# Transformer layer on one core: first modulation rows, dense weight chunks, decay vectors and norm vectors laid out by the host as one run per partition

## What is computed

```python
mod = silu(c) @ w_mod + b_mod                    # (1024) @ (1024, 6144), for c and c_ctx
sh1, sc1, g1, sh2, sc2, g2 = split(mod, 6)
h = ln_plain(x) * (1 + sc1) + sh1                # needs the first 2048 columns of w_mod
qa, ka, va, ra, af, ab, qd, kd, vd, ga, gb = split(h @ w_in)        # w_in (1024, 8224)
log_f = log_sigmoid(af @ w_alpha_f + b_alpha_f) / 16                # and the same backwards
# gated linear attention and differential attention side by side,
# merged = sigmoid(ga) * (o_a @ w_proj_a) + sigmoid(gb) * (o_d @ w_proj_b)
x = ln(alpha * x + g1 * (merged @ w_out))
# then 16 SwiGLU experts (2816 wide), each choosing its tokens
```

## Time and profile before

| | |
|---|---|
| median of 3 runs | 1785.42 us (1784.49 to 1785.57) |
| the profiled execution | 1784.7 us, of it span 1782.9 us |
| TensorE matmul busy | 1657.5 us, 93% of the span |
| VectorE, ScalarE, GpSimd busy | 512.3, 301.4, 56.1 us |
| moved by DMA | 638.74 MB, mean 358 GB/s; sync queue 54736 packets, GpSimd queue 3744 |
| granted TensorE clock | 0.98 of full speed |

### The profile page before, as it was taken

The page is one execution under the profiler, slowest core; times in us unless marked ns, Lnnn a source line. Parts: engine busy times, 40 slices in busy tenths (PEclk is TensorE's granted clock), DMA queues, the critical chain, the costliest instruction groups (busy, mean ns, idle before and its releaser), DMA issues.

```text
span 1782.9 us, 19120 instructions
## 1 busy us (share of the span) xinstructions
PE 1657.5 (93%) x7934; PEld 776.9 (44%) x7934; DVE 512.3 (29%) x979; ACT 301.4 (17%) x647; POOL 56.1 (3%) x91
## 2 busy tenths in 40 slices
PE   6999999999999999898988989898988989898997
PEld 3767777778873333332323232332323232333332
DVE  4575647765771111010101011010101011011041
ACT  3543354563331000000000000000000000000100
POOL 3110000021000000000000000000000000000000
PEclk9999999999999999999999999999999999999999
DMA  9962232237599999999999999999999999999997
GB/s 346 364 229 101 78 127 101 86 111 256 218 388 422 402 421 430 439 429 430 436 433 423 435 433 434 431 430 437 428 437 424 435 433 431 433 433 434 427 427 323
DMA packets 58528, 638.74 MB, mean 358 GB/s; under 512 B 5233, under 2 KB 5417, under 8 KB 36209
## 3 DMA queue, kind: packets, MB, share of 16 engines
q1 hardware_dynamic: 54736, 629.83, 84.4%
q0 software_dynamic: 3744, 8.26, 1.5%
HBM read 634.17 MB, written 3.90 MB: 358 GB/s over the span
## 4 chain that ended last, share of the span: by engine, by line
PE 57%; DMA 38%; SPq 2%; ACT 1%; DVE 1%; issue 0%; POOL 0%; POOLq 0%; ACTq 0%; DVEq 0%
PE banks L1401 25%; DMA ring<-in_w_exp_gate 19%; PE banks L970 18%; DMA ring<-in_w_exp_up 17%; PE banks L1536 3%; PE banks L1383 2%; DMA ring<-in_w_exp_down 2%; PE banks L968 1%; SPq L595 1%; DMA ring<-in_w_mod 1%; PE banks L921 1%; PE banks L1165 1%; PE banks L979 1%; PE banks L1186 1%; PE banks L966 1%; PE banks L1122 1%
## 5 line engine op out<-in xcount | busy, mean ns | idle before, releaser
L1401 PE MATMUL banks<-ring,O 128*64 128x512 f32 (+1 forms) x2844 | 635.0, 597 | 74.9 <-DMA ring<-in_w_exp_gate 53.4
L1401 PEld LDWEIGHTS banks<-ring,O 128*64 128x64 f32 x2844 | 199.1, 139 | 513.5 <-issue 413.4
L1536 PE MATMUL banks<-ring,O 128*64 128x512 f32 x1400 | 304.6, 593 | 7.5 <-ACT O L1884 6.7
L2459 DVE TENSOR_TENSOR X<-X,banks 128x512 f32<-128x512 f32 x90 | 61.8, 687 | 612.0 <-PE banks L1383 612.0
L970 PE MATMUL banks<-slot_parts,X_parts 128*128 128x512 f32 x672 | 191.1, 405 | 0.0
L1536 PEld LDWEIGHTS banks<-ring,O 128*64 128x64 f32 x1400 | 101.6, 137 | 199.4 <-issue 193.5
L970 PEld LDWEIGHTS banks<-slot_parts,X_parts 128*128 128x128 f32 x672 | 119.8, 188 | 32.3 <-issue 10.7
L1879 ACT ACTIVATE O<-banks 128x512 f32<-128x512 f32 (+1 forms) x48 | 23.7, 563 | 645.1 <-PE banks L1401 645.1
L2015 DVE TENSOR_TENSOR slot_parts<-ring,slot_parts 128x512 fp32r<-128x512 f32 x168 | 106.2, 694 | 14.1 <-ACT slot_parts L1591 13.7
L970 PE MATMUL banks<-slot_parts,H_parts 128*128 128x512 f32 x384 | 106.9, 391 | 0.0
L1591 ACT ACTIVATE O<-banks 128x128 f32<-128x128 f32 (+3 forms) x51 | 22.4, 439 | 494.5 <-PE banks L1312 388.9
(11 more groups left out here) (348 smaller groups left out, 1173.1 us busy)
## 6 DMA issues: line engine op xcount, KB each, us to landing
ring<-in_w_exp_up SPq DMA_DIRECT2D x26, 5632.0 KB, 28.5
ring<-in_w_exp_down SPq DMA_DIRECT2D x26, 4096.0 KB, 25.0
ring<-in_w_exp_gate SPq DMA_DIRECT2D x13, 5632.0 KB, 27.6
ring<-in_w_exp_gate SPq DMA_DIRECT2D x13, 4224.0 KB, 26.3
ring<-in_w_exp_down SPq DMA_DIRECT2D x15, 3072.0 KB, 22.5
ring<-in_w_in SPq DMA_DIRECT2D x16, 2048.0 KB, 8.8
ring<-in_w_exp_up SPq DMA_DIRECT2D x8, 2816.0 KB, 23.9
N<-in_w_exp_gate SPq DMA_DIRECT2D x15, 1408.0 KB, 30.4
```

The lines of the kernel that those rows point to most:

```text
L1401: x = pe.matmul(banks[64 * w:64 * w + 64, 3 * m + b, 0:(i1 - i0) * P], xeT[:, 2 * (k % 4) + k // 4, :], w4[:, w, i0 * P:i1 * P], start=(k ...
L1536: x = pe.matmul(banks[64 * w:64 * w + 64, (4 if last else 6) + dc, :], hidT[:, i, 64 * w:64 * w + 64], rows[:, w, dc * BANK:(dc + 1) * BAN ...
L2459: dve.tensor_tensor(dst, dst, banks[:, 3 + n % 3 if spread or last else 6 + n % 2, :], ALU.add).then_inc(acc_done, 1)
```

## The change

The host lays arrays out anew before the kernel is called (this is no part of the device time), and the loads read them so:

- first modulation rows: `w_mod0`, per half and partition one run in the order of the k-tiles; 4 loads of 1024 KB (runs of 8 KB) and 2 of 2048 KB (runs of 16 KB) take the place of 16 loads of 512 KB. The waits stand where they stood, with new counts;
- weight chunks: `w_chunks`, per chunk and partition one run of 16 KB;
- decay weights: `w_ab`, one run of 1 KB per partition in place of 8 of 128 bytes;
- decay biases: `b_alpha`, one load of 128 runs of 32 bytes in place of two loads;
- norm vectors: a run of 8 bytes and of 4 bytes per partition;
- the pieces read a `w_mod` without its first 2048 columns (row distance 16 KB in place of 24 KB); their runs stay 8 KB.

The order of all loads, their destinations and all arithmetic are as before.

```diff
@@ -269,8 +268,11 @@
         wpart = [x[:].rearrange("p (k n) -> p k n", k=KT) for x in slots_r]
 
 
+        def mod0_at(half, k):
+            return (2 * UNIT if half else WS0 + 2 * KT * BANK) + k * D
+
         def mod0_rows(half, k):
-            return reg((2 * UNIT if half else WS0 + 2 * KT * BANK) + k * D, D).rearrange("p (w n) -> p w n", w=2)
+            return reg(mod0_at(half, k), D).rearrange("p (w n) -> p w n", w=2)
 
         def tile_of(x, k):
             return x[:, k * BANK:(k + 1) * BANK]
@@ -556,9 +558,7 @@
                 eng.wait_ge(out, f[0] // 2 + n + 1)
 
         def w_chunk(n):
-            kind, c0 = WCHUNKS[n]
-            w = {"in": w_in, "pa": w_pa, "pb": w_pb, "out": w_out}[kind]
-            return w[0].rearrange("(k p) n -> p k n", p=P)[:, :, c0:c0 + BANK]
+            return w_chunks[n].rearrange("p (k n) -> p k n", k=KT)
 
         def wait_loaded(eng, n):
             eng.wait_ge(wsem[PAIR[n]], 16 * (len(before_in_pair(n)) + 1))
@@ -590,12 +590,12 @@
             sp.dma_start(x_r[:, 0, :], x_prompt[0]).then_inc(ld_x[0], 16)
             sp.dma_start(x_r[:, 1:3, :], x_sample[0].rearrange("(t p) d -> p t d", p=P)).then_inc(ld_x[1], 16)
 
-            def load_mod0(half, k):
-                rows0 = w_mod[0, k * P:(k + 1) * P, 0:2 * D].rearrange("p (w h n) -> p w h n", w=2, h=2)
-                sp.dma_start(mod0_rows(half, k), rows0[:, :, half, :]).then_inc(ld_mod0[half][k // (4 if half else 2)], 16)
-
-            for k in range(KT):
-                load_mod0(0, k)
+            def load_mod0(half, i):
+                n = 4 if half else 2
+                sp.dma_start(reg(mod0_at(half, i * n), n * D), w_mod0[half][:, i * n * D:(i + 1) * n * D]).then_inc(ld_mod0[half][i], 16)
+
+            for i in range(4):
+                load_mod0(0, i)
 
             def load_chunk(n):
                 if n == 0:
@@ -615,7 +615,7 @@
                     n = i % len(piece)
                     if i >= len(piece):
                         sp.wait_ge(piece_used, i - len(piece) + 1)
-                    sp.dma_start(piece[n], w_mod[0, k * P:(k + 1) * P, 2 * D * (b + 1):2 * D * (b + 2)]).then_inc(ld_piece[n], 16)
+                    sp.dma_start(piece[n], w_mod[k * P:(k + 1) * P, 2 * D * b:2 * D * (b + 1)]).then_inc(ld_piece[n], 16)
 
             def gate_up(w, e, q):
                 return gate_v[w][e].rearrange("(p k) f -> p k f", p=P)[:, 2 * q:2 * q + 2, :]
@@ -624,8 +624,8 @@
                 sp.dma_start(first_ups[k], gate_up(1, 0, 3)[:, k, :]).then_inc(land_u[3], 16)
 
             load_chunk(0)
-            for k in range(KT):
-                load_mod0(1, k)
+            for i in range(2):
+                load_mod0(1, i)
             load_pieces(0, 2)
             load_chunk(1)
             load_pieces(2, 6)
@@ -814,18 +814,17 @@
                     q = 32 * (2 * w + c)
                     pool.dma_start(mod_bias[0][q:q + 2, :].rearrange("p (h n) -> p h n", h=2),
                                    b_mod[:, w * D:(w + 1) * D].rearrange("o (h c n) -> o h c n", h=2, c=2)[:, :, c, :].to_broadcast((2, 2, 2 * P))).then_inc(ld_bm, 16)
-            pool.dma_start(wab, w_in[0].rearrange("(k p) n -> p k n", p=P)[:, :, C_AB:C_AB + 2 * RANK]).then_inc(ld_ab, 16)
+            pool.dma_start(wab, w_ab.rearrange("p (k n) -> p k n", k=KT)).then_inc(ld_ab, 16)
             pool.wait_ge(mod0_used, KT)
-            pool.dma_start(s("balpha", 0, 4), b_alpha_f[0].rearrange("(h p) -> p h", p=P)).then_inc(ld_wal, 16)
-            pool.dma_start(s("balpha", 4, 8), b_alpha_b[0].rearrange("(h p) -> p h", p=P)).then_inc(ld_wal, 16)
+            pool.dma_start(s("balpha", 0, 8), b_alpha).then_inc(ld_wal, 16)
             pool.wait_ge(mod0_used, KT + KT // 2)
             for g in range(4):
                 pool.dma_start(wal[32 * g:32 * g + RANK, 0:GH * DK], w_alpha_f[0]).then_inc(ld_wal, 16)
                 pool.dma_start(wal[32 * g + RANK:32 * g + 2 * RANK, GH * DK:2 * GH * DK], w_alpha_b[0]).then_inc(ld_wal, 16)
             pool.dma_start(resetm, k_r[0:1].to_broadcast((P, NT))).then_inc(ld_small, 16)
             pool.dma_start(km[:], k_m).then_inc(ld_small, 16)
-            pool.dma_start(s("gla_g"), gla_g[0].rearrange("(a p) -> p a", p=P)).then_inc(ld_small, 16)
-            pool.dma_start(s("sub_g"), sub_g[0].rearrange("(a p) -> p a", p=P)).then_inc(ld_small, 16)
+            pool.dma_start(s("gla_g"), gla_g).then_inc(ld_small, 16)
+            pool.dma_start(s("sub_g"), sub_g).then_inc(ld_small, 16)
             for i, v in enumerate((lq1, lk1, lq2, lk2)):
                 pool.dma_start(lamv[:, i * DH:(i + 1) * DH], v.to_broadcast((P, DH))).then_inc(ld_small, 16)
             for b in (1, 2):
@@ -940,7 +939,7 @@
                 elif kind == "al":
                     if i == 0:
                         wait_job_copied(pe, J_AB)
-                        pe.wait_ge(ld_wal, 16 * 10)
+                        pe.wait_ge(ld_wal, 16 * 9)
                     x = pe.matmul(out[:, 0:NT], wal[:, i * P:(i + 1) * P], abT, start=True, stop=True)
                 else:
                     a_hi, a_lo = {"pa": (oaT_high, oaT_low), "pb": (odT_high, odT_low),
@@ -998,9 +997,9 @@
 
                 out = banks[:, 7 - half, 0:2 * P]
                 if half and k % 4 == 0:
-                    pe.wait_ge(ld_mod0[1][k // 4], 64)
+                    pe.wait_ge(ld_mod0[1][k // 4], 16)
                 elif not half and k % 2 == 0:
-                    pe.wait_ge(ld_mod0[0][k // 2], 32)
+                    pe.wait_ge(ld_mod0[0][k // 2], 16)
                 for q in range(4):
                     w, c = divmod(q, 2)
                     x = pe.matmul(out[32 * q:32 * q + 32, :], cT[:, k, :], mod0_rows(half, k)[:, w, c * 2 * P:(c + 1) * 2 * P],
@@ -1955,7 +1954,7 @@
                     x = dve.tensor_copy(abT, b[:, 0:NT])
                 elif kind == "al":
                     if i == 0:
-                        dve.wait_ge(ld_wal, 160)
+                        dve.wait_ge(ld_wal, 16 * 9)
                     x = dve.tensor_scalar(LG4[:, i // GH, i % GH, :], b[:, 0:NT], s("balpha", i, i + 1), None, ALU.add)
                 elif kind == "pa":
                     x = dve.tensor_tensor(merged[:, i, cs], b, ga[:, i, cs], ALU.mult)
@@ -2516,10 +2515,25 @@
 ...
+def laid_out(inputs):
+    a = {n: np.asarray(x) for n, x in inputs.items()}
+    rows = {"in": a["w_in"], "pa": a["w_proj_a"], "pb": a["w_proj_b"], "out": a["w_out"]}
+
+    def by_partition(w):
+        return w.reshape(KT, P, -1).transpose(1, 0, 2).reshape(P, -1)
+
+    first = a["w_mod"][0][:, 0:2 * D].reshape(KT, P, 2, 2, BANK).transpose(3, 1, 0, 2, 4)
+    return {**a, "w_mod0": first.reshape(2, P, KT * D), "w_mod": a["w_mod"][0][:, 2 * D:],
+            "w_ab": by_partition(a["w_in"][0][:, C_AB:C_AB + 2 * RANK]),
+            "w_chunks": np.stack([by_partition(rows[w][0][:, c0:c0 + BANK]) for w, c0 in WCHUNKS]),
+            "b_alpha": np.concatenate([a[n][0].reshape(GH, P) for n in ("b_alpha_f", "b_alpha_b")]).T,
+            "gla_norm_g": a["gla_norm_g"][0].reshape(-1, P).T, "subln_g": a["subln_g"][0].reshape(-1, P).T}
 
 
 def kernel(**inputs):
@@ -2528,7 +2542,8 @@
 
     nc = _bacc.Bacc("TRN2", target_bir_lowering=False, num_devices=1, dynamic_dma_scratch_size=2048)
     arrays, args = {}, []
-    given = [(n, np.ascontiguousarray(inputs[n])) for n in _INS]
+    given = [(n, np.ascontiguousarray(a)) for n, a in laid_out(inputs).items() if n in _INS]
+    given.sort(key=lambda x: _INS.index(x[0]))
     given += list(zip(("const_f", "const_m", "const_r"), host_constants()))
     for name, a in given:
         arrays[f"in_{name}"] = a
```

More of the change, by code:

```diff
@@ L210, with trunk_layer @@
 FIRST_CUTS = {2: (4 * D,), 3: (DOWN0 + 8 * D - 3 * QUARTER,), 4: (DOWN0 + 14 * D - 4 * QUARTER,)}
-def trunk_layer(nc, x_prompt, x_sample, cache_k, cache_v, st_f, st_b, c, c_ctx, w_mod, b_mod, w_in,
-                w_alpha_f, b_alpha_f, w_alpha_b, b_alpha_b, gla_g, w_pa, lq1, lk1, lq2, lk2, sub_g, w_pb,
-                w_out, ln1_g, ln1_b, w_router, w_gate, w_up, w_down, ln2_g, ln2_b, k_f, k_m, k_r,
+def trunk_layer(nc, x_prompt, x_sample, cache_k, cache_v, st_f, st_b, c, c_ctx, w_mod0, w_mod, b_mod, w_ab, w_chunks,
+                w_alpha_f, w_alpha_b, b_alpha, gla_g, lq1, lk1, lq2, lk2, sub_g, ln1_g, ln1_b, w_router, w_gate, w_up, w_down, ln2_g, ln2_b, k_f, k_m, k_r,
                 y_all, new_k, new_v, new_f, new_b):
@@ L2518 @@
 _INS = ["x_prompt", "x_sample", "cache_diff_k", "cache_diff_v", "state_gla_fwd", "state_gla_bwd", "c", "c_ctx",
-        "w_mod", "b_mod", "w_in", "w_alpha_f", "b_alpha_f", "w_alpha_b", "b_alpha_b", "gla_norm_g", "w_proj_a",
-        "lambda_q1", "lambda_k1", "lambda_q2", "lambda_k2", "subln_g", "w_proj_b", "w_out", "ln1_g", "ln1_b",
+        "w_mod0", "w_mod", "b_mod", "w_ab", "w_chunks", "w_alpha_f", "w_alpha_b", "b_alpha", "gla_norm_g",
+        "lambda_q1", "lambda_k1", "lambda_q2", "lambda_k2", "subln_g", "ln1_g", "ln1_b",
```

(2 more changed lines are left out.)

## The result

| | before | after |
|---|---|---|
| median | 1785.39 us (1784.49 to 1786.29, 20 runs) | 1788.58 us (1786.72 to 1791.98, 20 runs) |
| profiled execution, of it span | 1784.7, 1782.9 us | 1788.9, 1787.0 us |
| packets of the sync queue | 54736 | 31536 |

The ratio is 1.0017, 95% interval 1.001 to 1.0023: the change makes the kernel slower, by 3.2 us. The forecast was 1781.9 and its range ended at 1785.4. The scatter of the runs has grown too, from 1.8 to 5.3 us.

What follows compares the result with a forecast made beforehand. The full sync queue was taken to bound the head, TensorE and expert weights the rest. Gains of 3.15 us at the last second-half modulation rows and 0.35 at piece 1 sum to 3.5: 1785.42 becomes 1781.9, range 1779.8 to 1785.4.

Steps and rivals of the forecast that it cites:

- rival B: Before L944: POOL's w_alpha loads become TensorE's stop, up to 2.4 us later, a stop of 1.3, 1783.2 us; chance 0.10.
- (1): Head, first modulation rows and chunk 0: 8 and 16 KB runs move at 425 to 429 GB/s; 2.5 us saved.
- (2): Head, decay biases: one load in place of two POOL loads removes the dip at 26 to 28 us; 0.5 us saved.
- (3): Head, decay weights: 128 runs of 1 KB in place of 1024 of 128 bytes; 0.15 us saved.
- (5): Sync queue's issues at L595: 6 in place of 16 save nothing, since the full queue makes them long.
- (6): Chunks 1 to 21: about 0.5 us saved per chunk, off the path because TensorE stays busy; gain nothing.
- (4): Norm vectors: two short POOL loads, waited for far later; gain nothing.
- (7): Pieces of w_mod: still 8 KB runs, only the row distance falls from 24 to 16 KB; gain nothing.
- A: Head: 389 GB/s is not due to run length; (1) gives 0 (1784.4 us) or half (1783.2); chance 0.13 for both.
- D: Head: power-of-two row distances read worse, slower below 375 GB/s; 1792.8 us at 296 GB/s; chance 0.07.
- E: Expert stage: tensors placed elsewhere change its rate, 2.9 us per GB/s, either sign; chance 0.06 of more than 2 us.
- C: Head: all disturbance goes, last modulation rows land by 34.0, TensorE's own work is the limit; 1781.0 us; chance 0.09.

Runs made afterwards that it cites:

- e2: The kernel after, with GpSimd's w_alpha loads moved ahead of its wait for TensorE's twelfth first-modulation tile; 1784.8 us.
- e7: The kernel after, with eleven matmuls whose results are unused put before TensorE's wait for the w_alpha loads; 1787.1 us.
- e9: The kernel after, with all 22 chunks read in 2 KB runs from contiguous arrays; 1783.0 us.
- e1: The kernel after, with chunk 1 alone read in 2 KB runs from a contiguous array; 1782.3 us.
- e6: The kernel after, with the w_alpha loads moved into the sync queue, behind pieces 0 and 1 and ahead of chunk 1; 1782.3 us.
- e5: The kernel after, with chunk 1 alone read in 256 runs of 8 KB; 1785.1 us.
- e8: The kernel after, with the w_alpha loads issued by ScalarE in its own queue, after TensorE's twelfth first-modulation tile; 1789.9 us.
- e11: The kernel before, with GpSimd's w_alpha loads moved ahead of its wait for TensorE's twelfth first-modulation tile; 1788.5 us.
- e3: The kernel before, layout untouched, with GpSimd's w_alpha loads held until TensorE's last first-modulation tile, the 16th and not the 12th; 1791.2 us.
- e10: The kernel before, layout untouched, with the w_alpha loads moved into the sync queue; 1785.3 us.

## Why the prediction was wrong

**The step that failed** is the price of rival B: "If each of these eight loads had to wait out one longer run of the sync queue [...] that is up to 8 x 0.3 = 2.4 us more: a stop of 1.3 at L944. 1783.2", with the reason against it, "the 5.8 were measured beside 8 KB runs, and these run beside the same pieces again". The sum itself had no term for a stop at L944. B had the mechanism and the place right, in part; its price and the reason against it were wrong. What the runs showed in their place is a stop of 3.40 us and up to 2.8 us of low clock behind it. Three things:

- "Beside 8 KB runs" and "beside the same pieces again" are where it went wrong. Before, the last load had 3.0 KB a packet beside it, since chunk 1's 2 KB runs moved from 41 us on; after, it had 9.2 KB, since the same chunk now came in 16 KB runs, and behind it the next pieces. I had checked who waits for chunk 1, nobody, and not who shares the DMA engines with it. Nor did "pieces, chunks and POOL loads are released by its own progress" hold for it: chunk 1 was issued 7.4 us earlier (22.55 against 29.91). The last landing took 9.62. B had 5.8 for it, the median of the earlier trace rows; the last of the eight took 6.2 in that trace, so the margin was 2.6 and not 3.0. B's upper bound was 5.8 + 2.4 = 8.2, 1.4 us too low. B counted one longer run for each load, 0.3 us more; but the eight landings are 0.6 us apart before (41.2 to 45.5) and 1.0 after (42.0 to 49.3), 0.4 more, and 1.4 in e2 (27.9 to 37.8).
- "Released 1.6 earlier" did not come. The last of the eight was issued at 39.71, 0.4 later than in the earlier trace rows. x lands at 2.42 + 6.5 = 8.9 in place of 8.3, and TensorE's first-half rows took 1.08 us for 8 matmuls where the earlier trace rows have 0.64; it was through with that half at 22.5 in place of 21.2. This is also where part of the gain for chunk 0 stayed: ScalarE, in the row below, is held by h until 25.79, not by chunk 0, which landed at 24.3. But e7 had the fast start, its last w_alpha load was issued at 37.35, and it landed 11.4 later, at 48.8 (after: 49.3). Issued 2.4 us earlier it landed 0.5 earlier: the missing 1.6 explain little of the stop.
- The clock was no term at all. A stop of 3.40 us costs 3.40, and then up to 2.8 us at 1.2 GHz (e7). B without it would have been 4.1 - 2.8 = 1.3 us slower, well inside the 3.6 us that the prediction took as its line; with it, 3.2 (medians) to 4.1 (profiled executions).

ScalarE's timeline of the kernel after, against the earlier trace rows:

```profile
23.93 1.86 ACT L1638 ACTIVATE H<-H,sm 128x128 f32<-128x128 f32 x4 [0.66 <-DVE sm L2029]
```

**What held.** (1) The rate: 424 GB/s from 8 to 35 us, the 425 to 429 of the forecast; last first-modulation rows at 34.5, forecast 34.9. (2), (3) The dips are gone, though 32 to 34 us has a new one, 373 at a share of 0.90. (5) Fewer issues: nothing seen on the path. (6) Chunks 1 to 21: nothing (e9), though the cover that I named, a TensorE that stays busy, was the wrong thing to look at. (4), (7): nothing seen, and not tried alone. The stop at piece 1 went (2.85 us gained there, forecast 3.5; in e7, which had the fast start, TensorE is 3.44 us ahead just behind it). With the collision taken away the layout gives 3.1 us (e1, e6), against 3.5.

**The rivals.** A (389 whatever the runs) is refuted by the rate. D (power-of-two distances) is refuted: 424 where it needed under 375. E is refuted: 431 again. C did not come; even e1 and e6 stay over 1782. The 3.7% that the prediction worked out, an estimate, from the 3 cycles a packet of the Trainium skill (DMA: Bandwidth & Descriptors, Why small descriptors are slow) is again below what was measured: 424 GB/s after, against 381 to 389 before in the slices from 20 to 26 us, is 9% or more.

**The chances.** Slower had 0.10, all of it on D and E. The outcome came by B, which I had put whole under "same" because its price stopped at 8 turns and had no clock in it.

**Open.** Why TensorE's first-half rows take 1.08 us in some profiled executions (after, e1, e9) and 0.64 in others (before, e5 to e8), with the granted clock given as 1.00 in both; e1 and e9 are among the fast kernels, so it doesn't decide here. How many turns a 32 KB load costs: the doses give an order, not a count. Why a stop of 2.5 us brings the clock down in one execution and not in another. And how much the earlier issue of chunk 1 adds: no run has its long runs without the faster queue in front of them.

## What to carry to other kernels

Longer runs make the bulk queue faster, but each small load of another queue then waits for longer runs, of every transfer that moves beside it and not only of those that somebody waits for. Before lengthening the runs, list the small loads that TensorE waits for with their margins, find out which transfers move beside them now and will then, with what runs, and put the urgent loads into the bulk queue or keep the runs beside them short. Take the margin from the last of these loads and not from the median. Price a stop of TensorE with the low clock behind it: stops of 1.9 to 5.0 us before the first up-projection cost 1.7 to 3.0 us more here.

## What the runs showed of the hardware that I had not expected

- A queue beside the bulk queue is late by the length of the bulk queue's runs. The last of eight 32 KB loads on GpSimd's queue took 5.9 to 6.4 us beside packets of 1.9 to 3.0 KB, 8.9 beside 7.6 KB, 9.6 to 12.6 beside 9.2 to 11.6 KB; on ScalarE's queue, with GpSimd's constants as a third party, 12 us.
- Eight loads of 32 KB (0.26 MB) beside a full queue cost it 0.8 to 1.1 MB (e11, e2), 2.1 to 2.6 us.
- After stops of 1.86 to 4.96 us (e5, after, e3, e8) TensorE ran at 1.2 GHz for some 4 to 7 us. From the first up-projection to L978 it took 11.9 us (e3, e5), 13.0 (after) and 13.2 (e8), against 10.2 without a stop.
- The same stop does not always bring the clock down: behind 2.50 us it stayed at 1.00 (before), behind 2.52 us at the same place it fell to 0.50 (e10).
